# A two-layer decoder trunk on one core: products on rows before LayerNorm is divided out, statistics gathered tile by tile

## The reference, cut to what matters

```python
def _layer_norm(x, g, b):
    mu = jnp.mean(xf, axis=-1, keepdims=True)
    var = jnp.mean(jnp.square(xf - mu), axis=-1, keepdims=True)
    y = (xf - mu) * lax.rsqrt(var + LN_EPS)
    return y * g + b

x = _layer_norm(ALPHA * x + mixer(x), ln1_g, ln1_b)
x = _layer_norm(ALPHA * x + (gelu(conv3(x @ W_gate)) * (x @ W_val)) @ W_down, ln2_g, ln2_b)
```

## Time and profile before

| what | value |
|---|---|
| median of the runs (range) | 1848.33 us (1843.23 to 1851.17) |
| the profiled execution's own time | 1850.55 us |
| its span, first to last instruction | 1848.3 us |
| mean granted TensorE clock | 0.978 |
| TensorE busy | 1757.2 us, 95% of the span |
| VectorE busy | 879.0 us, 48% |
| ScalarE busy | 521.4 us, 28% |
| GpSimd busy | 134.0 us, 7% |
| share of the chain that ended last: TensorE, VectorE, DMA, ScalarE, issue | 89%, 4%, 2%, 2%, 2% |

### The profile page before, as it was taken

How to read it: one execution, slowest core, us unless ns; L and a number is a source line. 1 busy time by engine, 2 the same in 40 slices (tenths; PEclk the granted TensorE clock), 3 DMA queues, 4 the chain that set the end, 5 groups by cost and what they waited for, 6 DMA issues and landing times.

```text
span 1848.3 us, 33928 instructions
## 1 busy us (share of the span) xinstructions
PE 1757.2 (95%) x12962; PEld 1572.6 (85%) x12962; DVE 879.0 (48%) x1406; ACT 521.4 (28%) x737; POOL 134.0 (7%) x121
## 2 busy tenths in 40 slices
PE   8999999989999999979999989989987999999996
PEld 8887456879999999979489679769856999999995
DVE  3236765465533554432552372272266655245544
ACT  3223442232222222232322222222224222122213
POOL 0000000010000000032104004014010100000000
PEclk9999999999999999989999999999998999999998
DMA  8997786212322322213332252343331323222321
GB/s 296 336 307 243 261 282 217 79 47 90 99 94 68 91 86 99 77 47 108 127 125 85 106 173 85 120 148 102 120 136 57 95 80 105 77 81 89 102 84 48
DMA packets 84072, 234.43 MB, mean 127 GB/s; under 512 B 9633, under 2 KB 9794, under 8 KB 83506
## 3 DMA queue, kind: packets, MB, share of 16 engines
q1 hardware_dynamic: 83138, 228.26, 37.2%
q0 software_dynamic: 880, 5.49, 0.8%
HBM read 209.90 MB, written 23.80 MB: 126 GB/s over the span
## 4 chain that ended last, share of the span: by engine, by line
PE 89%; DVE 4%; DMA 2%; ACT 2%; issue 2%; POOL 0%; SPq 0%; DVEq 0%; ACTq 0%; POOLq 0%
PE banks L1267 73%; PE banks L1496 2%; PE banks L1578 2%; PE banks L1298 2%; PE banks L1570 2%; PE banks L1405 1%; PE banks L1433 1%; PE banks L1558 1%; PE banks L1461 1%; DMA s<-in_s 1%; DVE x_lo L1040 1%; PE banks L1446 1%; DMA out_ret_s<-s 1%; PE banks L1534 1%; DVE y L1019 0%
## 5 line engine op out<-in xcount | busy, mean ns | idle before, releaser
L1267 PE MATMUL banks<-x_hi,w_hi 128*128 128x272 f32 x2624 | 550.8, 291 | 31.8 <-DVE x_lo L1040 21.8
L1267 PE MATMUL banks<-x_lo,w_hi 128*128 128x272 f32 x2624 | 545.5, 290 | 0.0
L1267 PE MATMUL banks<-x_hi,w_lo 128*128 128x272 f32 x2624 | 545.5, 289 | 0.0
L671 DVE TENSOR_TENSOR w_lo<-w_raw,w_hi 128x1024 fp32r<-128x1024 f32 (+2 forms) x228 | 278.3, 1221 | 523.7 <-ACT w_hi L443 523.2
L443 ACT ACTIVATE w_hi<-w_raw 128x1024 fp32r<-128x1024 f32 (+2 forms) x228 | 238.3, 1045 | 935.8 <-PE banks L1267 907.6
L1267 PEld LDWEIGHTS banks<-x_hi,w_hi 128*128 128x128 f32 x2624 | 415.0, 190 | 40.4 <-issue 27.9
L1267 PEld LDWEIGHTS banks<-x_lo,w_hi 128*128 128x128 f32 x2624 | 416.7, 190 | 0.0
L1267 PEld LDWEIGHTS banks<-x_hi,w_lo 128*128 128x128 f32 x2624 | 414.5, 190 | 0.0
L1267 PE MATMUL banks<-act_hi,w_lo 128*128 128x272 f32 x704 | 145.2, 287 | 0.0
L1267 PE MATMUL banks<-act_lo,w_hi 128*128 128x272 f32 x704 | 145.1, 287 | 0.0
L1267 PE MATMUL banks<-act_hi,w_hi 128*128 128x272 f32 x704 | 145.0, 287 | 0.0
(11 more groups left out here) (228 smaller groups left out, 1675.4 us busy)
## 6 DMA issues: line engine op xcount, KB each, us to landing
w_raw<-in_w_up SPq DMA_DIRECT2D x88, 512.0 KB, 3.5
kv<-in_kc SPq DMA_DIRECT2D x128, 256.0 KB, 4.4
kv<-in_vc SPq DMA_DIRECT2D x128, 256.0 KB, 4.4
w_raw<-in_w_rin SPq DMA_DIRECT2D x48, 512.0 KB, 3.5
w_raw<-in_w_dn SPq DMA_DIRECT2D x32, 704.0 KB, 4.0
s<-in_s SPq DMA_DIRECT2D x32, 512.0 KB, 6.8
out_ret_s<-s SPq DMA_DIRECT2D x32, 512.0 KB, 2.7
w_raw<-in_w_in_ab SPq DMA_DIRECT2D x20, 512.0 KB, 6.2
```

The source lines that it names most:

```text
L671: V.tensor_tensor(w_lo[:, j, 0:k * P], w_raw[:, j, 0:k * P], w_hi[:, j, 0:k * P].bitcast(F32), ALU.subtract).then_inc(lo_ready, 1)
L1267: last = mm(B[:, 2 * j + half, 0:HN], a[:, j, w], x[:, kt, half * HN:(half + 1) * HN], start=kt == 0 and n == 0, stop=kt == k - 1 and n == 2)
```

## The change

The high and low parts of the next product's input are made at once from the not yet normalised row, multiplied by LayerNorm's gain only. Two columns are added to the input, the gain and the shift, so the second column half has 274 columns where the product follows a LayerNorm, and the product yields for each output feature its sum over the gain and over the shift. At eviction a tile is multiplied by the inverse deviation of each position (rs), and (minus mean times rs) times the gain's sum plus the shift's sum is added (uf, ur). The statistics are sums of rows and of squared distances from a preliminary mean, taken from the first row tile; they are added up while the tiles of the product before are made, and TensorE makes the means behind the sixth contraction tile of the next product's first tile. ScalarE takes over the first tap of the convolution and loses the gate tile's copies; VectorE now empties the bank pairs. The pass of GpSimd over y has three operations a tile instead of one, and the retention's heads are written out four times instead of in a loop. The input of the first ConvFFN has buffers of its own. `log_k` changes a constant of the Newton step.

```diff
@@ GpSimd @@
-            def scale_residual(n):
-                pool.wait_ge(ln_done, n * KD + KD)
+            def scale_residual(n, base=None):
+                pool.wait_ge(ln_ready, n + 1)
+                rs, pm = RS[n], PM[n]
                 for m in range(KD):
-                    nc.gpsimd.tensor_scalar(y[:, m, :], y[:, m, :], lnp[:, n, 1, m:m + 1], ALPHA, ALU.add, ALU.mult)\
-                        .then_inc(y_scaled, 1)
-            scale_residual(0)
+                    if base is not None:
+                        pool.wait_ge(tile_done, base + 2 * m + 2)
+                    step.add(nc.gpsimd.tensor_tensor(y[:, m, :], y[:, m, :], rs, ALU.mult))
+                    step.wait()
+                    step.add(nc.gpsimd.tensor_tensor(halves(y[:, m, :]), halves(y[:, m, :]), pm, ALU.add))
+                    step.wait()
+                    if base is not None:
+                        pool.wait_ge(tile_done, base + 2 * m + 3)
+                    nc.gpsimd.tensor_scalar(y[:, m, :], y[:, m, :], lnp[:, n, 0, m:m + 1], lnp[:, n, 1, m:m + 1],
+                                            ALU.mult, ALU.add).then_inc(y_scaled, 1)
+            scale_residual(0, U_FFN[0])
             pool.wait_ge(y_scaled, KD)
             scale_residual(1)
...
@@ VectorE @@
+            def finish(n, base, k, k_next, scale=False):
...
+                for i in range(N_OUT):
+                    kk = k if i < N_OUT - 2 else k_next
+                    dve.wait_ge(tile_done, base + i + 1)
+                    out = halves(y[:, i, :])
...
+                        V.tensor_tensor(out, out, bank_pair(i % 2), ALU.add).then_inc(evicted[i % 2], 1)
+                    if i < N_OUT - 1:
+                        add_row(i)
+                        if kk:
+                            low(base + i + 2, i % 2, kk)
+                        low_row(i)
+                    if i == 3:
+                        dve.wait_ge(c_done, n + 1)
+                        step.add(V.tensor_scalar(halves(c), B[:, 4:6, 0:HN], float(KD), None, ALU.mult))
+                        shifted(0)
+                        shifted(1)
+                    elif i in (4, 5):
+                        for m in range(2 * i - 6, 2 * i - 4):
+                            add_square(m - 2)
+                            shifted(m)
+                    elif i == 6:
+                        add_square(4)
+                        shifted(6)
+                        add_square(5)
+                    elif i == 7:
+                        dve.wait_ge(evicted[1], (base + 7) // 2 + 2)
+                        shifted(7)
+                        add_row(7)
+                        add_square(6)
+                        low_row(7)
+                        add_square(7)
+                        step.wait()
+                        dve.sem_inc(s_sum, 1)
+                        if kk:
+                            low(base + 9, 1, kk)
+            def deviation(n, base):
...
+                V.tensor_tensor(halves(std[:, :]), B[:, 4:6, 0:HN], halves(c), ALU.subtract).then_inc(dm_ready, 1)
...
+                V.tensor_tensor(halves(v), B[:, 6:8, 0:HN], halves(std[:, :]), ALU.subtract).then_inc(v_ready, 1)
...
+                    low(base + 2, 0, KD)
                 dve.wait_ge(std_ready, n + 1)
+                step.add(V.tensor_tensor(c, std[:, :], std[:, :], ALU.mult))
...
+                step.add(V.scalar_tensor_tensor(c, v, eps, c, ALU.add, ALU.mult))
...
+                step.add(V.scalar_tensor_tensor(rs, c, 3.0 * NEWTON_K ** 2, std[:, :], ALU.subtract, ALU.mult))
...
+                    V.scalar_tensor_tensor(pm, B[:, 4:6, 0:HN], -1.0, halves(rs), ALU.mult, ALU.mult)                        .then_inc(ln_ready, 1)
...
+                    def pair(i, k, lead=False):
...
+                        V.tensor_scalar(col_f[:, 0, :], B[:, 1, HN:HN + 2], 1.0, None, ALU.mult).then_inc(col_ready, 1)
+                        V.tensor_tensor(halves(gc[:, 0:NT]), bank_pair(0), halves(rs_f[:, :]), ALU.mult)\
+                            .then_inc(evicted[0], 1)
...
+                        dve.wait_ge(u_ready, i * 2 + (2 * pairs + 1))
...
+                        step.add(V.tensor_tensor(gp[:, 2:2 + TP], gc[:, 0:TP], uf[:, 0:TP], ALU.add))
...
+                        if not lead:
+                            low(i * 2 + (base + 2), 0, k)
...
-            ffn(0, KD)
-            norm(1)
-
-            dve.wait_ge(y_scaled, 2 * KD)
+            ffn(0)
+            finish(1, U_FFN[0] + 2 * N_UP + N_OUT, KF, KD)
+            deviation(1, U_RET)
             dve.wait_ge(zeroed, 5)
             step.add(V.memset(rmv[:, :, :], 1.0))
...
+                    V.tensor_scalar(col_r[:, :], B[:, 2 * j + 1, HN:HN + 2], 1.0, None, ALU.mult)\
+                        .then_inc(rcol_ready, 1)
+                    V.tensor_tensor(halves(dst), bank_pair(j), halves(RS[1]), ALU.mult).then_inc(evicted[j], 1)
+                    dve.wait_ge(ru_ready, h * N_RIN + i + 1)
+                    dve.wait_ge(evicted[j], u // 2 + 2)
+                    V.tensor_tensor(dst, dst, ur[:, :], ALU.add).then_inc(rin_ready, 1)
+                    if h or i:
+                        low(u + 2, j, KD if i < N_RIN - 2 else 4)
...
@@ ScalarE, the retention's input tiles @@
+                    act.wait_ge(rcol_ready, h * N_RIN + i + 1)
...
+                    nc.scalar.activation(halves(ur[:, :]), PM[1], ACT.Identity, scale=col_r[:, 0:1],
+                                         bias=col_r[:, 1:2]).then_inc(ru_ready, 1)
+                    if not first:
+                        split(base + (i + 2), i % 2, KD if i < N_RIN - 2 else 4)
+                    if i >= 8:
+                        act.wait_ge(rin_ready, h * N_RIN + i + 1)
+                        nc.scalar.activation(dst, dst, ACT.Silu)
...
@@ TensorE @@
+            def finish(n, base, k, hi, lo, k_ready=None):
+                for i in range(N_OUT):
+                    tile(base + i, k, hi, lo, k_ready if i == 0 else None)
+                    if i == 2:
+                        pe.wait_ge(evicted[0], base // 2 + 2)
+                        for half in range(2):
+                            last = mm(B[:, 4 + half, 0:HN], mean_mat, y[:, 0, half * HN:(half + 1) * HN],
+                                      start=True, stop=True)
+                        last.then_inc(c_done, 1)
+            def means(n):
                 pe.wait_ge(s_sum, n + 1)
...
+                for bank, rows in ((4, s1[:, :]), (6, SQUARES[n])):
+                    for half in range(2):
+                        last = mm(B[:, bank + half, 0:HN], mean_mat, rows[:, half * HN:(half + 1) * HN],
+                                  start=True, stop=True)
                 last.then_inc(m_done, 1)
```

More of the change, by code:

```diff
@@ L20 @@
 HN = NT // 2
+NX = NT + 2
 NB = TP // P
@@ L84, in loop @@
     @contextmanager
-    def loop(self, reg, times, per):
-        first = self.n
+    def loop(self, reg, begin, end, per):
+        first = self.n = self.n - begin * per
         self.loops.append((reg, per))
@@ L90, in loop @@
         assert self.n - first == per, f"{self.n - first} steps a turn, not {per}"
-        self.n = first + per * times
+        self.n = first + per * end
 def uses(slot):
@@ L329, in _ @@
             load_ffn(0)
-            with sp.Fori(0, H_C) as h:
+            for h in range(H_C):
                 base = h * N_RET + U_RET
@@ L598, in ffn @@
+                        split(i * 2 + (base + 3), 1, k)
+                    pair(0, KD, half == 0)
+                    with act.Fori(1, KF - 1) as i:
                         pair(i, KD)
                     pair(KF - 1, KF)
[L600 to L606 removed]
@@ L608, in _ @@
-            splits(U_OUT_AB, N_OUT, KD, KD)
-            norm(0)
-            ffn(0, KD)
-            norm(1)
+                    if half == 0:
+                        splits(base + N_UP, N_OUT, KF, KD)
+            finish(0, U_OUT_AB, KD, KD)
+            deviation(0, U_FFN[0])
+            ffn(0)
+            finish(1, U_FFN[0] + 2 * N_UP + N_OUT, KF, KD)
+            deviation(1, U_RET)
             nc.scalar.preload_act_table_set("silu_and_others")
-            with act.Fori(0, H_C) as h, step.loop(h, H_C, 0):
+            for h in range(H_C):
@@ L1263, in tile_body @@
                         k_ready(kt)
+                    if between and kt == 6:
+                        between()
                     w = slice(kt * P, (kt + 1) * P)
                     for n, (a, x) in enumerate(((w_hi, hi), (w_hi, lo), (w_lo, hi))):
-                        for half in range(2):
-                            last = mm(B[:, 2 * j + half, 0:HN], a[:, j, w], x[:, kt, half * HN:(half + 1) * HN],
+                        for half, cols in enumerate((slice(0, HN), slice(HN, width))):
+                            last = mm(B[:, 2 * j + half, 0:cols.stop - cols.start], a[:, j, w], x[:, kt, cols],
                                       start=kt == 0 and n == 0, stop=kt == k - 1 and n == 2)
@@ L1489, in norm @@
+            def means(n):
```

(13 more changed lines are left out.)

414 lines of the change are left out of this document (242 added, 172 removed).

## The result

The changed kernel takes 1855.5 us (median of 13 runs, 1851.2 to 1858.4) beside 1847.8 for the kernel before on the same chip: 1.0043 times as long, 95% interval 1.0033 to 1.0053. It is slower by 6 to 10 us, where 14 us less was forecast. The profiled execution took 1857.36 us, its span is 1855.6.

A forecast was written before the change was run, and what follows sets the result against it. TensorE, busy 95% of the span, was taken as the bound, so only its waits around the LayerNorms (103 us) could be won. Terms 16.7 - 7.0 + 8.5 + 4.0 - 4.6 - 3.0 gave 14.6 us less: 1834 us, range 1825 to 1843.

The forecast's parts named there:

- Wider matmuls: Two more columns in 136 tiles of 24 matmuls, priced in proportion to width: 3.0 us lost.
- The pairs: 44 pairs of up-projection tiles: VectorE's added work, about 3 us each, fits under TensorE's tiles, 1.9 us spare; costed at nothing.
- the tail: Last LayerNorm (norm 3) at the kernel's end: VectorE's final pass starts earlier; 4.0 us saved.
- norm 0: First LayerNorm, ahead of a ConvFFN: TensorE's wait falls from 22.8 us; 16.7 us saved.
- norm 1: LayerNorm before the heads: VectorE waits for GpSimd's longer pass and memset, third input tile at T + 44.7; 7.0 us lost.
- norm 2: LayerNorm before the second ConvFFN, held by VectorE: 25.1 us falls to 16.6; 8.5 us saved.
- GpSimd blocks VectorE: Rival: in sixteen pairs VectorE loses all of GpSimd's 3.5 us a tile, 25.6 us late in all: 1859 us; chance 0.08.
- VectorE bounds all pairs: Rival: gaps between VectorE's dependent operations make all 44 pairs half a microsecond late, 22 us: 1856 us; chance 0.10.
- the heads: Behind each head's twelfth input tile ScalarE's table load begins later, 1.15 us in each of four: 4.6 us lost.
- hold isn't there: Rival: at the LayerNorm before the heads GpSimd's pass ends before VectorE needs it, 32 us less: 1802 us; chance 0.05.

The follow-up runs named there:

- Experiment 5: The kernel before with the rows of the split product inputs 546 elements apart instead of 544, nothing else changed: 1855.2 us, ratio 1.0048.
- experiment 4: The changed kernel with VectorE subtracting the mean from all eight row groups in the last LayerNorm, GpSimd from none: 1852.3 us, ratio 1.0029.
- experiment 3: The changed kernel with GpSimd's rope load and clearing of qm moved ahead of its 24 scalings of the residual: 1825.5 us, ratio 0.9881.

## Why the prediction was wrong

The largest step that failed is **Wider matmuls**, with **The pairs** behind it. It priced two columns by the column, at 3.0 us, and that price was nearly right (3.6 us, about 0.5 ns a column against 125.3 / 272 = 0.46). What it left out is that the same edit, `NX = NT + 2`, lays every row of the input 2184 bytes apart instead of 2176. "No wait, no operation" was taken for "no cost"; the bounds from none to 0.92 ns were bounds of a wider matmul, not of a matmul on other addresses, and the term was counted for 3264 matmuls where every matmul on these tensors pays. Experiment 5 has it alone in the kernel before: 9 us, 5.9 to 11.8 by its interval. Layer 0's second set of tensors got a start of its own besides; in the changed kernel distance and start together cost 6.2 us.

The second failure is **the tail**, nearly as large: 4.0 saved was forecast, 1.5 was lost. The prediction allowed 0.3 us for GpSimd's company there, from the earlier trace rows, where one pass of 7.25 us had cost VectorE about 1.6. Those operations of VectorE's mostly did not meet GpSimd's; in the tail each does, and 4.9 us went: 1.8 in the two subtractions, 3.1 in the three Newton steps, by the rows of experiment 4.

What no term had: the lower granted clock behind norm 0, 1.6 us (the forecast took it only behind norm 1 and, at 0.4, behind norm 2, where it was 1.6 too). Head 0's 3.6 us come in some executions and not in others.

**GpSimd blocks VectorE** as a rival was wrong by place. In the pairs the same thing happens, but to one or two operations a pair. The addition at L1203 with GpSimd's pass beside it, then without:

```profile
L1203 DVE TENSOR_TENSOR af<-af,ge x7: 1730/1732/1733, 395.7 to 468.8; 128x512 f32<-128x512 f32 x7
...
L1203 DVE TENSOR_TENSOR af<-af,ge x7: 691/691/692, 607.8 to 680.9; 128x512 f32<-128x512 f32 x7
```

1.04 us lost of 1.9 spare: a pair takes 12.19 us with and without it. The forecast's "0.8 of its 1.9: nothing" held. The rival would have been worth weighing for the tail, where nothing covers it, rather than for the pairs.

**VectorE bounds all pairs** is out: TensorE has no idle time in them, and with other addresses and the same VectorE a pair takes 12.08. The prediction's sign for it, longer tiles in the up products, came (6.1 us for 6.0), but from the rows and the columns.

Right: **norm 0** (15.7 for 16.7), **norm 1** (the third tile at T + 45.3 for T + 44.7, and behind it the granted clock at 0.63 for 5 us), **the heads** (3.8 for 4.6), **norm 2** in kind (6.7 for 8.5). The rival **hold isn't there** is out by experiment 3, which shows that the hold costs 30 us. These four add up to -12.0 where -13.6 was forecast. So the forecast's reading of these stages stood. Of the 21.8 us between -14.6 and the +7.2 of the two profiled executions, 6.2 are a cost in no stage, on the engine that is busy 95% of the time, 5.5 the tail, 3.6 head 0, 3.2 the clock behind norms 0 and 2, 1.8 norm 2; none of them alone turns the sign.

```profile
785.00:816.00 31.00, 0.46 (x2) 0.49 (x3) 1.11 (x4) 0.84 (x1) 27.79 (x26) 0.56 0.04 10
816.00:821.00 5.00, 5.00 (x28) 5.00 (x28) 4.20 (x5) 1.79 (x2) 2.75 (x2) 0.63 0.15 56
```

(Busy time by stretch of the changed kernel, columns as in the earlier trace rows: the hold, in which GpSimd alone works, and the 5 us behind it.)

What stays open: the rule by which start and distance of rows set the spacing of matmuls, and with it the price of a column, which the runs give at 0.3 to 0.7 ns by the address.

## What to carry to other kernels

When an edit enlarges a tensor that the busiest engine reads, ask where its rows then lie, and pad them back to the distance they had, or measure that edit alone in the old kernel: a nanosecond in each of thousands of matmuls shows in no wait and cost nearly what the change saved at one LayerNorm here. A queue's order can be worth more than arithmetic: a load and a memset moved ahead of 24 operations gave 30 us. A gain and a loss of the same size in the total prove nothing of each other: compare the starts of the same instructions, stretch by stretch. Work shared out to GpSimd beside VectorE costs VectorE its own time wherever no cover is left, as at the end of a kernel.

## What the runs showed of the hardware that was not expected

- Matmuls of 272 columns come 125.3 ns apart with rows 2176 or 2240 bytes apart and 0.8 ns later with 2184 (a tile of 48: 6.20 and 6.21 against 6.25 us; a pair of 96: 12.00 to 12.05 against 12.09 to 12.11).
- With rows of 2240 bytes, tensors that begin 32 bytes behind a multiple of 64 cost 0.1 us a pair of 274-column tiles (12.18 against 12.08); with rows of 2304 bytes the same start cost nothing (12.08).
- VectorE operations of two operands on chip memory that run beside GpSimd's of the same kind take 1.73 to 1.85 us instead of 0.72 to 0.78, 1.0 us more, where GpSimd's takes 1.33 alone and 1.70 beside them.
